# Splitting the decay scores of an RWKV-7 block into array quadrants, with two other pieces of work moved behind later steps

## The chip, the cores and the metric

The kernel runs on one core of one Trainium2 chip. The metric is the device time of one execution in microseconds. Before the change three runs gave 1024.06, 1024.72 and 1024.76 us, so the median is 1024.72 us.

## The reference, cut to what matters

One layer of a hybrid model works on 512 tokens of width 1024. It has a projection `w_in`, an RWKV-7 time mix with 16 heads of 64, a sliding-window attention, two gated output projections and a convolutional feed-forward block. The change sits in the time mix, whose recurrence is

```python
def step(S, inp):
    r_t, w_t, k_t, v_t, aa_t, bb_t = inp
    sa = jnp.einsum('bhvk,bhk->bhv', S, aa_t)
    S = S * w_t[:, :, None, :] + sa[..., None] * bb_t[:, :, None, :] + v_t[..., None] * k_t[:, :, None, :]
    y_t = jnp.einsum('bhvk,bhk->bhv', S, r_t)
    return S, y_t
...
y = (y - mean) * lax.rsqrt(var + GN_EPS)
y = y.reshape(B, T, RWKV_DIM) * lnx_w.astype(f32) + lnx_b.astype(f32)
bonus = jnp.sum(rh * kh * r_k.astype(f32), axis=-1, keepdims=True) * vh
y = (y + bonus.reshape(B, T, RWKV_DIM)) * g.astype(f32)
```

The kernel computes it in chunks of 128 tokens. Inside a chunk it needs, for each head, the scores of every key (the vectors b and k, scaled by decays) against every query (a and r, scaled likewise), kept only where the query is later than the key. The part of b against a is a triangular matrix N, and the kernel needs the inverse of (1 - N).

## The kernel before, in words

The heads are worked off two at a time, in eight pairs n = 0 to 7; head h of a pair lies on partitions 64h to 64h + 63. The 512 tokens are four chunks j. For each pair the kernel runs three stages, on TensorE (`pe`), VectorE (`dve`), ScalarE (`act`) and GpSimd (`pool`), each with an order written out by hand and semaphores between them:

- `scores(n)`: 16 fp32 matmuls (each shown in the profile as two passes) of a chunk's 128 keys (`bp` or `kp`, 64 rows) against its 256 queries (`ar`: 128 for a, then 128 for r). They fill the PSUM banks 0 to 5 and then 0 and 1 again. VectorE moves them out in eight `copy_predicated` under the mask `causal` (`masked`, L1532): `gb` holds the scores of b, `gk` those of k, and what the mask leaves out stays zero from one clearing at the start. TensorE also turns value, `bp` and `kp` chunks by transposes (`turned`, L2232).
- `invert(n)`: ScalarE copies N to fp16 (`n1`, `score_copy`, L1073), and GpSimd subtracts to get the rounding error (`n2`, `remainder`, L738). Then seven levels double the size of the inverted blocks of Y and of its transpose X. VectorE makes X's first level (`xx`, L1582) and Y's first level (`yy`, two masks, L1597); each later level is a product (L2351), a mask (`v1`, L1597), a product (L2374) and a sum (`yy`, L1608).
- `scan(n)`: the chain over the four chunks, run at the start of the next pair.

Between these pieces TensorE runs one k-step (three matmuls, L2046 to L2048) or two of the tiles of `w_in` that are still to be projected, by a table `FILL` of places ("scores", "centred", "tokens", (level, "masks"), ...). VectorE and ScalarE split those tiles' weights in high and low parts (L1357; in halves L1569 at levels 1, 2, 4 and 5).

The norm of the pair before (d = n - 1) is threaded through this. TensorE sums squares by row (`norm_var`, L2226), ScalarE takes the root (`deviation`: `brow` and `yrow`), TensorE turns it (`turned_var`, L2277), VectorE divides and spreads the result over 512 columns (`deviations`, L1520 and the copy L1507), TensorE turns it back (`deviations`, L2232 of `ysq`), and `scaled_output` uses it at level 3. GpSimd sends the bonus rows through DRAM and back (`bonus_back`: L814, L817), fetches the next key norms (`key_norms_in`, L808) and multiplies (L850).

Of the kernel before, what the change touches and what calls it, by code (L numbers as in the profile page):

```python
# [31 lines left out]
U32 = mybir.dt.uint32  # L32
# [22 lines left out]
SCORE_BANK = (0, 1, 2, 3, 4, 5, 0, 1)  # L55
# [67 lines left out]
def build(nc, x, norm1_g, w_in, rwkv_mu, w0, w2, a0, a2, g2, k_k, k_a, r_k, lnx_w, lnx_b,  # L123
          b_qkv, attn_sink, gate_b, w_proj_a, w_proj_b, w_out, norm2_g, w_up, conv_w,
          conv_b, w_down, normf_g, out):
    with ExitStack() as ctx:
# [149 lines left out]
        gb = take("gb", [P, NT, 2, 2 * C])  # L276
# [3 lines left out]
        gk = take("gk", [P, NT, 2, 2 * C])  # L280
# [356 lines left out]
        def _(pool):  # L637
# [98 lines left out]
            def remainder(n):  # L736
                pool.wait_ge(n1_ready, n + 1)
                pool.tensor_tensor(n2[:, :, :, :], gb[:, :, :, 0:C], n1[:, :, :, :], ALU.subtract)\  # L738
                    .then_inc(n2_ready, 1)
# [96 lines left out]
            for n in range(1, PAIRS):  # L836
# [6 lines left out]
                odd_columns(n)  # L843
                remainder(n)
                bonus_back(n - 1)
# [39 lines left out]
        def _(act):  # L885
# [185 lines left out]
            def score_copy(n):  # L1071
                act.wait_ge(g_ready, n * 8 + 4)
                act.activation(n1[:, :, :, :], gb[:, :, :, 0:C], ACT.Copy).then_inc(n1_ready, 1)  # L1073
# [277 lines left out]
        def _(dve):  # L1351
# [171 lines left out]
            def masked(n, f):  # L1523

                j0, h = (f % 4) // 2 * 2, f % 2
                dst = (gb, gk)[f // 4][:, j0:j0 + 2, h, :]
                if n == 0:
                    dve.wait_ge(cleared, 1 + f // 4)
                dve.wait_ge(g_ps, n * 8 + f + 1)

                dve.memset(carrier[:, f:f + 1], 0.0)
                dve.copy_predicated(dst, causal[:, :].bitcast(U32).unsqueeze(1)  # L1532
                                    .to_broadcast([P, 2, 2 * C]),
                                    ps[SCORE_BANK[f]][:, :].rearrange("p (j t) -> p j t", j=2))\
                    .then_inc(g_ready, 1)
# [42 lines left out]
            def invert(n, d, following):  # L1578
# [7 lines left out]
                for lv in range(LEVELS):  # L1586
                    for g in range(2):
                        dve.wait_ge(v_ps, n * (2 * LEVELS) + (2 * lv + g + 1))
                        vg = v1[:, 2 * g:2 * g + 2].rearrange("p j h t -> p (j h t)")
                        if lv == 0:  # L1590
# [126 lines left out]
            for f in range(8):  # L1717
                masked(0, f)
            value_tokens(0)
            invert(0, None, True)  # L1720
            for n in range(1, PAIRS):
# [305 lines left out]
        def _(pe):  # L2027
# [251 lines left out]
            def scores(n, d, fill):  # L2279
# [4 lines left out]
                for f in range(0, 8, 2):  # L2284
                    src, j0 = (bp, kp)[f // 4], f % 4
                    if f == 6:
                        pe.wait_ge(g_ready, n * 8 + 2)
                    for j in range(j0, j0 + 2):
                        for h in range(2):
                            hs = slice(h * HD, (h + 1) * HD)  # L2290
                            ins = pe.matmul(ps[SCORE_BANK[f + h]][:, (j - j0) * 2 * C:  # L2291
                                                                  (j - j0 + 1) * 2 * C],
                                            src[hs, j * C:(j + 1) * C], ar[hs, 1 - n % 2, j, :],
                                            start=True, stop=True)
                            if j > j0:
                                ins.then_inc(g_ps, 1)
                if d is not None:
# [16 lines left out]
            def invert(n, d, following, fill):  # L2314
# [20 lines left out]
                for lv in range(LEVELS):  # L2335
# [5 lines left out]
                    for g in range(2):  # L2341
# [415 lines left out]
```

## Time and profile before

| | us |
|---|---|
| median of three runs | 1024.72 |
| the profiled execution's own time | 1024.05 |
| its span, from the first to the last instruction | 1022.3 |
| TensorE busy | 1011.7 |
| VectorE busy | 738.1 |
| ScalarE busy | 516.2 |
| GpSimd busy | 224.4 |

The profile's times are counted from the start of the span; 1.75 us of the execution's own time lie outside it. In the timeline a row has its start, its length and the instruction, with the number of like instructions merged (x16) and, in brackets, the engine's idle time before it. A TensorE row's length includes the way through the array, so the rate of matmuls is read from one start to the next.

### The profile page before, as it was taken

How to read it: one execution, taken by the hardware profiler on the slowest of the kernel's cores; microseconds unless marked ns; L12 is line 12 of the kernel's file. 1: busy time of each engine (PE TensorE's matmuls, PEld its weight loads, DVE VectorE, ACT ScalarE, POOL GpSimd, SP SyncE). 2: the span in 40 equal slices, each digit the busy share in tenths (PEclk: the TensorE clock that was granted, in tenths of full speed). 3: DMA queues.
4: the chain of work that ended last, by engine and by line, in shares of the span. 5: the costliest groups of instructions: out<-in, count | busy, mean ns of one | idle time of the engine just before them, and what ended most of it. 6: DMA issues, size and time to landing. Idle time of an engine off the chain costs nothing.

```text
span 1022.3 us, 18746 instructions
## 1 busy us (share of the span) xinstructions
PE 1011.7 (99%) x7106; PEld 806.3 (79%) x7106; DVE 738.1 (72%) x1233; ACT 516.2 (50%) x869; POOL 224.4 (22%) x298
## 2 busy tenths in 40 slices
PE   8999999999999999999999999999999999999997
PEld 7888888777777777777777888888888888888886
DVE  5224667788988888888877565367767777789786
ACT  6435756844435445345453322264455444467744
POOL 7642355330221422413210554000000000000000
PEclk9999999999999999999999999999999999999999
DMA  6874456331303313214255867613233333337662
GB/s 187 233 236 153 132 191 215 94 76 43 86 25 74 86 63 87 61 60 120 93 164 153 238 234 258 198 40 103 85 102 92 95 100 103 92 114 226 203 189 113
DMA packets 161291, 133.25 MB, mean 130 GB/s; under 512 B 32729, under 2 KB 137735, under 8 KB 161223
## 3 DMA queue, kind: packets, MB, share of 16 engines
q1 hardware_dynamic: 147687, 88.41, 29.7%
q0 software_dynamic: 13520, 43.90, 13.9%
q8 instruction: 47, 0.77, 0.3%
q14 instruction: 21, 0.17, 0.0%
q10 hardware_dynamic: 16, 0.00, 0.0%
HBM read 111.83 MB, written 20.45 MB: 129 GB/s over the span
## 4 chain that ended last, share of the span: by engine, by line
PE 94%; DVE 2%; DMA 1%; issue 1%; ACT 1%; POOL 0%; SPq 0%; DVEq 0%; POOLq 0%; ACTq 0%
PE ps L2090 14%; PE ps L2093 14%; PE ps L2092 14%; PE ps L2046 6%; PE ps L2048 5%; PE ps L2047 5%; PE ps L2677 3%; PE ps L2678 3%; PE ps L2679 3%; PE ps L2291 3%; PE ps L2425 2%; PE ps L2232 2%; PE ps L2613 1%; PE ps L2611 1%; PE ps L2612 1%; PE ps L2374 1%
## 5 line engine op out<-in xcount | busy, mean ns | idle before, releaser
L1357 DVE TENSOR_TENSOR wlo<-raw,whi 128x1024 fp32r<-128x1024 f32 x106 | 140.1, 1322 | 125.9 <-ACT whi L893 108.0
L893 ACT ACTIVATE whi<-raw 128x1024 fp32r<-128x1024 f32 x116 | 122.6, 1057 | 127.0 <-PE ps L2093 116.0
L2090 PE MATMUL ps<-xnh,whi 128*128 128x512 f32 x336 | 130.7, 389 | 0.0
L2092 PE MATMUL ps<-xnl,whi 128*128 128x512 f32 x336 | 130.7, 389 | 0.0
L2093 PE MATMUL ps<-xnh,wlo 128*128 128x512 f32 x336 | 130.7, 389 | 0.0
L2046 PE MATMUL ps<-xh,whi 128*128 128x512 f32 x192 | 89.5, 466 | 0.0
L2090 PE MATMUL ps<-xh,whi 128*128 128x512 f32 x224 | 88.3, 394 | 0.0
L2092 PE MATMUL ps<-xl,whi 128*128 128x512 f32 x224 | 87.3, 390 | 0.0
L2093 PE MATMUL ps<-xh,wlo 128*128 128x512 f32 x224 | 87.2, 389 | 0.0
L2048 PE MATMUL ps<-xh,wlo 128*128 128x512 f32 x192 | 76.1, 396 | 0.0
L2047 PE MATMUL ps<-xl,whi 128*128 128x512 f32 x192 | 75.3, 392 | 0.0
L2090 PEld LDWEIGHTS ps<-xnh,whi 128*128 128x128 f32 x336 | 63.1, 188 | 13.2
L2092 PEld LDWEIGHTS ps<-xnl,whi 128*128 128x128 f32 x336 | 63.1, 188 | 13.2
L2093 PEld LDWEIGHTS ps<-xnh,wlo 128*128 128x128 f32 x336 | 63.1, 188 | 13.0
L1093 ACT ACTIVATE xx<-ps 128x256 f16<-128x256 f32 x96 | 32.1, 381 | 69.1 <-PE ps L2331 68.3
L2090 PEld LDWEIGHTS ps<-xh,whi 128*128 128x128 f32 x224 | 42.0, 188 | 10.1 <-issue 0.8
L2093 PEld LDWEIGHTS ps<-xh,wlo 128*128 128x128 f32 x224 | 42.1, 188 | 8.9
L2092 PEld LDWEIGHTS ps<-xl,whi 128*128 128x128 f32 x224 | 42.1, 188 | 8.4
L1879 DVE TENSOR_TENSOR sq<-ps,rs 128x512 f32<-128x512 f32 x44 | 30.4, 691 | 23.5 <-PE ps L2093 18.5
L745 POOL TENSOR_TENSOR z<-z,kmod 128x512 f32<-128x512 f32 x8 | 16.2, 2025 | 126.2 <-DVE kp L1488 126.2
L2048 PEld LDWEIGHTS ps<-xh,wlo 128*128 128x128 f32 x192 | 36.0, 188 | 8.3
L1608 DVE TENSOR_TENSOR yy<-ps,yy 128x256 f16<-128x256 f32 x96 | 36.2, 419 | 8.6 <-PE ps L2374 8.3
(430 smaller groups left out, 2454.6 us busy)
## 6 DMA issues: line engine op xcount, KB each, us to landing
raw<-in_w_in SPq DMA_DIRECT2D x108, 256.0 KB, 3.3
raw<-in_w_up SPq DMA_DIRECT2D x88, 256.0 KB, 3.0
wrow<-in_w_down POOLq DMA_DIRECT2D x22, 512.0 KB, 5.1
raw<-weight_scratch SPq DMA_DIRECT2D x44, 256.0 KB, 3.4
raw<-in_w_down SPq DMA_DIRECT2D x32, 256.0 KB, 2.9
weight_scratch<-wrow POOLq DMA_DIRECT2D x11, 512.0 KB, 3.1
gates_scratch<-gst POOLq DMA_DIRECT2D x16, 256.0 KB, 3.2
raw<-in_w_proj_b SPq DMA_DIRECT2D x16, 256.0 KB, 4.2
```

Of the source, the lines that this page charges most:

```text
L893: act.activation(flat(whi[:, hb]), flat(raw[:, b]), ACT.Copy).then_inc(w_hi, 1)
L1093: act.activation(dst, src, ACT.Copy).then_inc(x_ready, 1)
L1357: dve.tensor_tensor(flat(lo[:, hb]), flat(raw[:, b]), flat(hi[:, hb]).bitcast(F32), ALU.subtract).then_inc(w_lo, 1)
L1608: dve.tensor_tensor(yg, low_half(ps[2 * g][:, :], lv), yg, ALU.add)\
L2046: pe.matmul(o, whi[:, hb, k, :], self.hi(k), start=k == 0, stop=False)
L2047: pe.matmul(o, whi[:, hb, k, :], self.lo(k), start=False, stop=False)
L2048: ins = pe.matmul(o, wlo[:, hb, k, :], self.hi(k), start=False, stop=k == KT - 1)
L2090: pe.matmul(ps[bank][:, :], whi[:, hb, k, :], hi(k), start=first and k == 0, stop=False)
L2092: pe.matmul(ps[bank][:, :], whi[:, hb, k, :], lo(k), start=False, stop=False)
L2093: ins = pe.matmul(ps[bank][:, :], wlo[:, hb, k, :], hi(k), start=False, stop=last and k == kn - 1)
L2291: ins = pe.matmul(ps[SCORE_BANK[f + h]][:, (j - j0) * 2 * C: (j - j0 + 1) * 2 * C], src[hs, j * C:(j + 1) * C], ar[hs, 1 - n % 2, j, :], s ...
L2677: pe.matmul(o, h_hi, hi[:, cols], start=start, stop=False)
```

## The change

It has four parts.

1. The scores of the early 64 keys of a chunk against its early 64 queries (of a and r) become matmuls of 64 x 64 that lie in the four quadrants of the array: head h picks the rows, the parity e of the chunk picks the output partitions. They fill banks 2 and 3, for b and k together. The late 64 queries are scored against all 128 keys in banks 0, 1 (b) and 4, 5 (k). The early queries against the late keys, which the mask cleared, are not computed. No bank is used twice. There are 32 matmuls (64 passes) where there were 16 (32 passes), each with 128 moving columns instead of 256.
2. VectorE moves them out in eight `copy_predicated` again: four on 64 partitions for the early queries (two of these read partitions 64 to 127 and write 0 to 63), then two late ones for b, then the value tokens, then two late ones for k. All of b's scores are complete after the sixth, where they were after the fourth. In pair 0 the first of them waits until `gk` is cleared too.
3. The norm's division and its spreading (`deviations` on VectorE) move from between the masks to behind the two masks of Y's first level; TensorE's turning back moves from the scores to level 1, ahead of the fill (1, "masks"). `turned_var` moves behind the turns of values and `bp`.
4. GpSimd sends the bonus rows ahead of its subtraction, and the subtraction waits until X's first level is made (`x_start`).

```diff
+EARLY_BANK = (2, 3)
+LATE_BANK = ((0, 1), (4, 5))
...
-        gb = take("gb", [P, NT, 2, 2 * C])
+        gg = take("gg", [P, NT, 2, 2, 2, C])
+        gb, gk = (gg[:, 2 * i:2 * i + 2].rearrange("p x e h q t -> p (x e) h (q t)")
+                  for i in range(2))
...
             def remainder(n):
                 pool.wait_ge(n1_ready, n + 1)
+                pool.wait_ge(x_start, n + 1)
...
                 odd_columns(n)
+                bonus_back(n - 1)
                 remainder(n)
-                bonus_back(n - 1)
...
             def score_copy(n):
-                act.wait_ge(g_ready, n * 8 + 4)
+                act.wait_ge(g_ready, n * 8 + 6)
...
+            def late_masked(n, i, h):
+                f = 4 + 2 * i + h
                 if n == 0:
-                    dve.wait_ge(cleared, 1 + f // 4)
+                    dve.wait_ge(cleared, 1 + i)
                 dve.wait_ge(g_ps, n * 8 + f + 1)
...
+            def early_masked(n, h, e):
+                if n == 0:
+                    dve.wait_ge(cleared, 2)
+                dve.wait_ge(g_ps, n * 8 + 4)
+                predicated(gg[0:HD, :, e, h, :, 0:C // 2],
+                           two_parts(causal[0:HD, :], slice(0, C // 2)),
+                           ps[EARLY_BANK[h]][e * HD:(e + 1) * HD, :]
+                           .rearrange("p (x q t) -> p x q t", x=NT, q=2),
+                           None if h or e else 0)
...
+                    if lv == 0 and d is not None:
+                        deviations(d)
...
-                for f in range(6):
-                    masked(n, f)
-                deviations(n - 1)
-                for f in range(6, 8):
-                    masked(n, f)
+                masked(n, 0)
                 value_tokens(n)
+                masked(n, 1)
                 invert(n, n - 1, n < PAIRS - 1)
...
+                def late(i):
+                    src = (bp, kp)[i]
+                    for j in range(NT):
+                        for h, hs in enumerate(rows):
+                            ins = pe.matmul(ps[LATE_BANK[i][h]][:, j * C:(j + 1) * C]
+                                            .rearrange("p (q t) -> p q t", q=2),
+                                            src[hs, j * C:(j + 1) * C], both(hs, j, slice(HD, C)),
+                                            start=True, stop=True)
...
+                        for e in range(2):
+                            j = 2 * jj + e
+                            for h, hs in enumerate(rows):
+                                ins = pe.matmul(ps[EARLY_BANK[h]][e * HD:(e + 1) * HD, o:o + C]
+                                                .rearrange("p (q t) -> p q t", q=2),
+                                                src[hs, j * C:j * C + HD], both(hs, j, slice(0, HD)),
+                                                start=True, stop=True)
...
                 fill("scores")
-                if d is not None:
-                    turned_var(d)
-                pe.wait_ge(g_ready, n * 8 + 3)
+                pe.wait_ge(g_ready, n * 8 + 2)
                 turned(2, z[:, n + 16, :]).then_inc(tok_ps, 1)
                 pe.wait_ge(g_ready, n * 8 + 4)
                 turned(3, bp).then_inc(tok_ps, 1)
                 if d is not None:
-                    deviations(d)
+                    turned_var(d)
                 fill("centred")
-                pe.wait_ge(g_ready, n * 8 + 8)
+                pe.wait_ge(g_ready, n * 8 + 6)
                 turned(1, kp).then_inc(tok_ps, 1)
...
+                    if lv == 1 and d is not None:
+                        deviations(d)
                     fill((lv, "masks"))
```

## Rows read from the trace of the kernel before

**Rows 1.** The page, busy us of each engine and its instructions.

```profile
PE 1011.7 (99%) x7106; PEld 806.3 (79%) x7106; DVE 738.1 (72%) x1233; ACT 516.2 (50%) x869; POOL 224.4 (22%) x298
```

**Rows 2.** Timeline of TensorE in pair 4, from the scores to level 1.

```profile
376.24 2.00 PE L2291 MATMUL ps<-ar,bp 64*128 64x256 f32 x16
...
379.91 0.43 PE L2226 MATMUL ps<-ysq,meancols 128*32 128x128 f32 x8
380.15 0.40 PE L2226 MATMUL ps<-z,rkcols 128*32 128x128 f32 x8
...
382.32 0.66 PE L2232 MATMUL ps<-ident,ysq 128*128 128x128 f32 x4
382.74 0.48 PE L2046 MATMUL ps<-xh,whi 128*128 128x512 f32 x1
...
386.77 0.42 PE L2351 MATMUL ps<-yy,n 128*128 128x64 f16 x8
...
387.80 0.42 PE L2374 MATMUL ps<-v,xx 128*128 128x64 f16 x8
```

**Rows 3.** Timeline of VectorE in pair 4, from the first mask to level 1.

```profile
377.41 0.74 DVE L1532 COPY_PREDICATED gb<-causal,ps 128x512 f32<-128x512 uint32 x1 [0.29 <-issue]
...
380.57 0.75 DVE L1532 COPY_PREDICATED gk<-causal,ps 128x512 f32<-128x512 uint32 x1
...
381.60 0.21 DVE L1520 RECIPROCAL ystd<-ps 128x8 f32<-128x8 f32 x1 [0.28 <-PE ps L2277]
381.84 0.43 DVE L1507 COPY ysq<-ystd 128x512 f32<-128x512 f32 x1
...
383.50 0.67 DVE L1497 TENSOR_REDUCE vsum<-ps 128x8 f32<-128x512 f32 x1
...
384.81 0.69 DVE L1582 TENSOR_TENSOR xx<-n,first_level 128x1024 f16<-128x1024 f16 x1
385.41 0.78 DVE L1597 TENSOR_TENSOR yy<-ps,level_mask 128x256 f16<-128x256 f32 x2
...
388.80 0.68 DVE L1569 TENSOR_TENSOR wlo<-raw,whi 128x512 fp32r<-128x512 f32 x1
```

**Rows 4.** Timeline of TensorE, the attention's scores and the next product.

```profile
184.41 1.16 PE L2176 MATMUL ps<-kb,qc 64*128 64x128 f32 x16
185.51 0.50 PE L2090 MATMUL ps<-xh,whi 128*128 128x512 f32 x1
```

**Rows 5.** Timelines of VectorE and GpSimd where their instructions meet.

```profile
221.67 1.49 DVE L1582 TENSOR_TENSOR xx<-n,first_level 128x1024 f16<-128x1024 f16 x1
...
220.43 2.17 POOL L738 TENSOR_TENSOR n<-gb,n 128x1024 f16<-128x1024 f32 x1
...
160.91 1.63 DVE L1414 TENSOR_SCALAR nmx<-mx 128x8 f32<-128x8 f32 x1
...
161.20 1.30 POOL L781 TENSOR_TENSOR wrow<-wrow 128x512 f32<-128x512 f32 x1
```

**Rows 6.** Timeline of VectorE in pair 1, the last step before the masks.

```profile
254.67 0.75 DVE L1392 SCALAR_TENSOR_TENSOR z<-ps,par,z 128x511 f32<-128x511 f32 x1
...
255.33 0.74 DVE L1532 COPY_PREDICATED gb<-causal,ps 128x512 f32<-128x512 uint32 x1
```

**Rows 7.** Timeline of GpSimd in pair 4, the bonus rows.

```profile
384.27 0.56 POOL L814 DMA_DIRECT2D bonus_scratch<-brow  x1
386.38 1.26 POOL L817 DMA_DIRECT2D z<-bonus_scratch  x2 [1.54 <-DMA bonus_scratch<-brow]
...
392.03 1.29 POOL L850 TENSOR_TENSOR z<-z 128x512 f32<-128x512 f32 x1 [3.15 <-DMA z<-bonus_scratch]
```

**Rows 8.** Timeline of pair 0: the first mask, the clearing, level 1.

```profile
215.24 0.73 DVE L1532 COPY_PREDICATED gb<-causal,ps 128x512 f32<-128x512 uint32 x1
215.26 1.88 POOL L829 MEMSET gk<- 128x2048 f32 x1
...
223.84 0.44 PE L2351 MATMUL ps<-yy,n 128*128 128x64 f16 x8
```

More of the change, by code:

```diff
@@ L54 @@
 FILL_BANK = (7, 4, 7)
-SCORE_BANK = (0, 1, 2, 3, 4, 5, 0, 1)
+EARLY_BANK = (2, 3)
+LATE_BANK = ((0, 1), (4, 5))
 WARM = 24
@@ L279, in build @@
         ysb = take("ysb", [P, T])
-        gk = take("gk", [P, NT, 2, 2 * C])
         rkcols = take("rkcols", [P, P // NT])
@@ L1521, in deviations, with two_parts, predicated, masked @@
                 spread(ysq, ystd).then_inc(vex_ready, 1)
-            def masked(n, f):
-                j0, h = (f % 4) // 2 * 2, f % 2
-                dst = (gb, gk)[f // 4][:, j0:j0 + 2, h, :]
+            def two_parts(t, ts):
+                return t.rearrange("p (q t) -> p q t", q=2)[:, :, ts]
+            def predicated(dst, mask, scores, f=None):
+                if f is not None:
+                    dve.memset(carrier[:, f:f + 1], 0.0)
+                dve.copy_predicated(dst, mask.bitcast(U32).unsqueeze(1)
+                                    .to_broadcast([mask.shape[0], NT, 2, C // 2]), scores)\
+                    .then_inc(g_ready, 1)
+            def late_masked(n, i, h):
+                f = 4 + 2 * i + h
                 if n == 0:
-                    dve.wait_ge(cleared, 1 + f // 4)
+                    dve.wait_ge(cleared, 1 + i)
                 dve.wait_ge(g_ps, n * 8 + f + 1)
[L1531 to L1535, printed above, removed]
+                predicated((gb, gk)[i][:, :, h, :].rearrange("p j (q t) -> p j q t", q=2)
+                           [:, :, :, C // 2:], two_parts(causal[:, :], slice(C // 2, C)),
+                           ps[LATE_BANK[i][h]][:, :].rearrange("p (j q t) -> p j q t", j=NT, q=2), f)
+            def early_masked(n, h, e):
[7 more added lines that the diff above has]
+                           None if h or e else 0)
+            def masked(n, i):
+                if i == 0:
+                    for h in range(2):
+                        for e in range(2):
+                            early_masked(n, h, e)
+                for h in range(2):
+                    late_masked(n, i, h)
             def add_bonus(d):
@@ L1716, in _ @@
             weights(n + 2)
-            for f in range(8):
-                masked(0, f)
+            masked(0, 0)
             value_tokens(0)
+            masked(0, 1)
             invert(0, None, True)
@@ L2283, in scores, with both @@
                     pe.wait_ge(ps_free, N_FILL - 1)
[L2284 to L2293, printed above, removed]
+                rows = [slice(h * HD, (h + 1) * HD) for h in range(2)]
+                def both(hs, j, ts):
+                    return ar[hs, 1 - n % 2, j, :].rearrange("p (q t) -> p q t", q=2)[:, :, ts]
+                def late(i):
[5 more added lines that the diff above has]
+                                            src[hs, j * C:(j + 1) * C], both(hs, j, slice(HD, C)),
                                             start=True, stop=True)
-                            if j > j0:
+                            if j == NT - 1:
                                 ins.then_inc(g_ps, 1)
+                for i, src in enumerate((bp, kp)):
+                    for jj in range(2):
+                        o = (2 * i + jj) * C
+                        for e in range(2):
+                            j = 2 * jj + e
[4 more added lines that the diff above has]
+                                                start=True, stop=True)
+                                if i and jj:
+                                    ins.then_inc(g_ps, 1)
+                late(0)
+                late(1)
                 if d is not None:
```

## Prediction

> **What bounds the kernel now.** I read the page first: TensorE is busy 1011.7 us of a span of 1022.3 us [rows 1], so a change is worth what it takes from TensorE's own work, less what TensorE then has to wait. Next I read one pair in the timeline, engine by engine; pair 4 stands for pairs 3 to 7. On TensorE the scores start at 376.24, the variance products follow at 379.91, level 1's first product starts at 386.77 and its second at 387.80 [rows 2]. The reader is to see that each of these starts where the matmuls ahead of it end: nothing in this stretch waits for long. On VectorE the first mask starts at 377.41 and Y's first level ends at 386.19 [rows 3], 0.58 before level 1 needs it. VectorE is close behind TensorE all the way, and that is the margin which the change moves. The profiled execution took 1024.05 us by itself, 0.67 below the median of the runs; my sums are made against 1024.05.
>
> **Part 1, the quadrants.** Before, the 32 passes of the scores hold TensorE for 3.67 us (379.91 - 376.24) [rows 2], the change of tile shape behind them included. After, the 32 late passes have the shape of the attention's scores: 16 of those take 1.10 us to the next product's start [rows 4], of which I allow 0.2 for the change of shape between them, so 0.056 each and 1.8 us. The 32 early passes use half the rows and half the columns, and no row shows that. From below: the variance products use a quarter of the columns and eight of them take 0.24 us (380.15 - 379.91) [rows 2], so 0.03 each and 0.96 us. From above: no more than two at a time, 0.056 each, 1.8 us. I take 0.96, because the variance products show four streams at once and a quadrant needs four. With 0.4 for two changes of shape the scores take 3.16 us, which frees 0.51 us of each pair (with the upper bound they take 4.0, a loss of 0.3). The turning of `ysq`, 0.42 us (382.74 - 382.32) [rows 2], leaves this stretch and comes back at level 1.
>
> **Part 2, the masks.** Eight masks stay eight, at 0.63 us from start to start (five steps from 377.41 to 380.57) [rows 3]. The first early mask needs all 32 early passes, so it starts a little later: before, the first increment came with the sixth pass, which starts 5 x 0.11 = 0.55 after the first (3.67 / 32 = 0.11); after, the last comes with the 32nd, which starts 31 x 0.03 = 0.93 after the first. That is 0.38 later, less some 0.1 for a pass of half the columns, so the mask starts 0.28 later, at 377.69. In pairs 1 and 2 the first mask starts when the shift ends (255.33 against 255.42) [rows 6], and nothing is lost there. Two early masks read partitions 64 to 127, which no mask before does; I price that at nothing, by the nearest row, the masks that follow each other at 0.63, and keep as the upper bound the loss of the overlap of two neighbours (0.74 - 0.63 = 0.11) at each of four changes of partitions, 0.44 a pair.
>
> From there VectorE's chain in pair 4 is a plain sum. The sixth mask ends at 377.69 + 5 x 0.63 + 0.75 = 381.59; value tokens from 381.50, with 1.31 from their start to that of what follows (384.81 - 383.50) [rows 3]; masks 7 and 8 from 382.81, and X's first level from 384.10 to 384.79. The copy of N by ScalarE has to wait for mask 6 instead of mask 4, but X's first level comes 2.5 us later than that mask, so it is not late. Y's first level ends at 385.48. This is 0.7 us earlier than before, since the division has left the chain.
>
> **Parts 3 and 4, where they meet.** Now the division (0.21) and the spreading copy (0.43) [rows 3] stand behind Y's first level, and the copy would run from 385.64 to 386.07. But GpSimd's subtraction is released by X's first level, so it runs in the same stretch: from about 384.84 for 2.17 [rows 5], to 387.01. GpSimd is free for it: the variance products now end before 380, and the bonus rows need 2.11 + 1.26 = 3.37 us from first issue to the last one [rows 7], so they are sent off by 384.8 if they start by 381.4.
>
> What happens when VectorE and GpSimd meet is in [rows 5]. In pair 0 X's first level took 1.49 us instead of 0.69 [rows 3]; it started inside the subtraction and ended 0.56 behind its end (223.16 against 222.60). At 160.91 an instruction on eight columns with a single tensor took 1.63 us and ended with GpSimd's instruction (162.54 against 162.50). Both sat out GpSimd's work. The spreading copy is of the second kind: one tensor, SBUF to SBUF, and at 0.43 for 512 columns faster than the 0.68 of a two-tensor step of the same size [rows 3]. So I expect the copy to end at 387.01 + 0.30 = 387.31 (its 0.43 less the 0.13 which the held X also had behind it). The masks of level 1 read PSUM and stand behind it in VectorE's queue.
>
> The Trainium skill, "VectorE: DVE Perf Modes", section "Mode 2×_2P — use both read ports for one tensor", says that an fp32 copy within SBUF doubles its rate by using the second read port too, and its section "Two Vector instructions with no wait between them" calls that read interface shared with GpSimd. By that the copy is held as [rows 5] show for its neighbours; were a copy with a repeated source exempt, the sum would be that of the first rival.
>
> TensorE stands waiting for this copy at level 1: it reaches the place near 386.1 (386.77 less the 0.51 and 0.42 that left, plus some 0.25 for the product), and can turn `ysq` only after 387.31. From there the turn (0.42), the fill (1.03 from first to second product [rows 2], less the product) and a semaphore's way make 1.27; the second product starts at 388.58 against 387.80 [rows 2]: 0.78 us later in each of pairs 3 to 7, and 0.50 in pairs 1 and 2. The 0.51 us which the quadrants free is waited away there.
>
> **What comes late next.** GpSimd fetches key norms once `ysq` is turned (two issues like the 1.26 of [rows 7], from about 388.1) and then multiplies the bonus (1.29) from about 389.4; its rows have landed (5.65 us from the issue at 386.38 to 392.03 [rows 7], now issued near 382.8). Before, that multiplication ran at 392.03, away from any step it could hold. Now the half-weight split of level 1 comes at 388.58 + 1.00 = 389.6 (388.80 - 387.80) [rows 2, 3]: two SBUF tensors, like those held in [rows 5]. If GpSimd is first by these 0.2 us, the split ends 0.55 behind 390.7 instead of at 390.3; 0.95 late. Part of that is slack, as the 0.58 ahead of level 1 was; between nothing (with the split first, too) and 0.95 I take 0.7, since by the sum GpSimd is first, in pairs 1 to 6 (pair 7 fetches no key norms).
>
> **Pair 0** has no norm to divide, but its first mask now waits for the clearing of `gk`, until 215.26 + 1.88 = 217.14 instead of 215.24 [rows 8]. X's first level ends 7.1 us behind the first mask (384.79 - 377.69), at 224.3, Y's at 225.0; level 1's product comes at about 225.0 instead of 223.84: 1.2 us. The 0.8 us that X lost to the subtraction there is no gain, because TensorE did not wait for it.
>
> **The sum.** 5 x 0.78 + 2 x 0.50 + 6 x 0.7 + 1.2 = 10.3 us, so 1034.3 against 1024.05. I state 1034.5 for the measured median, between this and the same sum on 1024.72.
>
> **The rivals.**
> - *The split goes first.* Without the 0.7 at level 2: 6.1 us, 1030.2. For it: the lead is 0.2 us, within the error of a sum of seven durations. Against it: nothing shown.
> - *The copy is not held (the other side).* Then it ends at 386.07, the second product starts at 386.1 + 1.27 = 387.4, so 0.4 earlier in pairs 3 to 7 and 0.7 in pairs 1 and 2: 1.2 - 2.0 - 1.4 = -2.2, 1021.8. It decides as soon as the subtraction starts later than 385.6, that is when the bonus rows keep GpSimd until then, or when a copy can run beside GpSimd. Against it: both held steps of [rows 5]. With masks at their upper bound this case gives 1024.9, no change.
> - *Masks held at a change of partitions.* 0.44 in each of seven pairs on top of the forecast: 3.1, 1037.4. It delays the chain that sets the end, so it counts in full. The Trainium skill's "VectorE: DVE Perf Modes", section "Two Vector instructions with no wait between them", has such a rule: an instruction whose input starts in another quadrant of partitions than the last one waits until all before it are finished. No row here shows it.
> - *The quadrants overlap only two at a time.* The masks start 31 x 0.026 = 0.8 later in pairs 3 to 7: 4.0 more, 1038.3. Against it: the 0.03 of [rows 2].
>
> **How the numbers follow.** The forecast 36 in 100, the split first 24, the copy not held 28 (18 of these faster by over 0.2%, 10 within), masks held 6, two quadrants 6. A change of 0.2% is 2 us, about what these runs can tell. The range runs from 1022, which leaves out the better part of the second rival, to 1038, which leaves out the last: some 2 in 10 lie outside. The likeliest case's own range, with the split first or not and masks half held, is 1030 to 1036. So faster 0.18, within 0.2% 0.10, slower 0.72.
>
> **What the profile after will show.** Right: the scores about 0.5 us shorter; the spreading copy 1.6 us long instead of 0.43, ending with the subtraction; TensorE idle over 1 us ahead of turning `ysq` at level 1; in pairs 1 to 6 the first half-weight split longer than 0.68. Wrong: a copy of 0.43 beside the subtraction, or a subtraction that starts behind it; then the time falls below 1024. If the early passes start 0.056 apart, the last rival holds; if early masks start more than 0.7 apart, the third.

## The result and the profile after

The kernel got slower: 1043.80 us median (1042.49 to 1044.44, four runs) against 1024.74 us for the kernel before on the same chip, a ratio of 1.0186, 95% interval 1.0174 to 1.0198. The profiled execution took 1044.17 us, with a span of 1042.5. The prediction had the direction right, but said 1034.5 us with a range up to 1038: some 10 us more where 19 were measured.

The page of the kernel after, the line that answers to [rows 1]:

```profile
PE 1012.4 (97%) x7362; PEld 809.4 (78%) x7362; DVE 756.0 (73%) x1209; ACT 516.6 (50%) x869; POOL 223.3 (21%) x298
```

TensorE is as busy as before in a span that is 20.2 us longer, so it waits. VectorE is busy 18 us longer with 24 instructions fewer: single instructions of it have grown. Where TensorE waits, in the view of the waits (total, number, longest; the DMA's and other single waits of the start left out):

```profile
PE ps L2257 <- DVE ysq L1510: 11.7, 7, 2.0
PE ps L2416 <- DVE v L1623: 3.4, 5, 0.8
...
PE ps L2257 <- DVE gg L1532: 2.0, 2, 1.1
PE ps L2071 <- ACT n L1076: 1.8, 7, 0.4
```

Four waits: for the spread norm `ysq`, turned at level 1, in each of the seven pairs; for the mask `v` of level 2; for the masks of pair 0; and for ScalarE's copy of N. The last of them costs nothing, because it comes ahead of the wait for `ysq` in the same pair: without it TensorE would stand that much longer for `ysq`. The timeline of TensorE in pair 4 shows where they lie (it answers to [rows 2]):

```profile
386.40 0.67 PE L2331 MATMUL ps<-ar,bp 64*64 64x128 f32 x16
386.89 0.62 PE L2331 MATMUL ps<-ar,kp 64*64 64x128 f32 x16
387.43 1.16 PE L2318 MATMUL ps<-ar,bp 64*128 64x128 f32 x16
388.43 1.06 PE L2318 MATMUL ps<-ar,kp 64*128 64x128 f32 x16
389.42 0.43 PE L2251 MATMUL ps<-ysq,meancols 128*32 128x128 f32 x8
...
393.27 0.50 PE L2071 MATMUL ps<-xh,whi 128*128 128x512 f32 x1 [0.20 <-ACT n L1076]
...
397.99 0.66 PE L2257 MATMUL ps<-ident,ysq 128*128 128x128 f32 x4 [1.58 <-DVE ysq L1510]
...
399.19 0.41 PE L2416 MATMUL ps<-v,xx 128*128 128x64 f16 x8
...
402.44 0.62 PE L2416 MATMUL ps<-v,xx 128*128 128x64 f16 x8 [0.80 <-DVE v L1623]
402.90 0.47 PE L2071 MATMUL ps<-xh,whi 128*128 128x512 f32 x1
```

The scores did get shorter: 3.02 us from their start to the variance products (389.42 - 386.40) against 3.67. The 16 early passes of b take 0.49 us to those of k (386.89 - 386.40), 0.031 each. That is half of the 0.062 of a late pass of the same 128 columns ((388.43 - 387.43) / 16), whose 64 x 128 tile fits into the array twice; so four quadrants do run at once. But behind them TensorE stands 0.20, 1.58 and 0.80 us: 2.58 in this pair. VectorE in the same pair (answers to [rows 3]):

```profile
387.66 0.72 DVE L1532 COPY_PREDICATED gg<-causal,ps 64x512 f32<-64x512 uint32 x1 [0.38 <-issue]
...
388.41 2.29 DVE L1532 COPY_PREDICATED gg<-causal,ps 64x512 f32<-64x512 uint32 x3
...
390.74 1.38 DVE L1532 COPY_PREDICATED gg<-causal,ps 128x512 f32<-128x512 uint32 x2
...
394.64 0.65 DVE L1608 TENSOR_TENSOR xx<-n,first_level 128x1024 f16<-128x1024 f16 x1
395.23 0.76 DVE L1623 TENSOR_TENSOR yy<-ps,level_mask 128x256 f16<-128x256 f32 x2
395.90 0.17 DVE L1523 RECIPROCAL ystd<-ps 128x8 f32<-128x8 f32 x1
396.11 1.82 DVE L1510 COPY ysq<-ystd 128x512 f32<-128x512 f32 x1
...
400.19 1.86 DVE L1595 TENSOR_TENSOR wlo<-raw,whi 128x512 fp32r<-128x512 f32 x1
```

and GpSimd (answers to [rows 7]):

```profile
390.96 0.54 POOL L817 DMA_DIRECT2D bonus_scratch<-brow  x1 [1.23 <-ACT yrow L1047]
394.22 1.26 POOL L820 DMA_DIRECT2D z<-bonus_scratch  x2 [2.73 <-DMA bonus_scratch<-brow]
395.49 2.15 POOL L741 TENSOR_TENSOR n<-gg,n 128x1024 f16<-128x1024 f32 x1
...
400.19 1.31 POOL L853 TENSOR_TENSOR z<-z 128x512 f32<-128x512 f32 x1
```

Read the two side by side. The spreading copy (1.82 instead of 0.43) lies beside the subtraction and ends 0.29 behind it (397.93 against 397.64). The split (1.86 instead of 0.68) starts with GpSimd's multiplication and ends 0.55 behind it (402.05 against 401.50). TensorE waits for the copy itself, and behind the split for the mask `v`, which stands next in VectorE's queue. In all seven pairs the copy ends 0.28 to 0.29 behind the subtraction, so the start of the subtraction sets how long TensorE waits. The early masks are a second thing: from the first of them to the first late one 3.08 us pass in four steps (390.74 - 387.66), 0.77 each, against 0.63 before.

Windows of one pair, from scores to scores (us; busy time and instructions of PE, PEld, DVE, ACT, POOL; granted clock; DMA share; GB/s), first the kernel before, pair 4:

```profile
376.24:416.86 40.62, 40.62 (x477) 30.18 (x475) 34.31 (x82) 19.01 (x39) 10.95 (x13) 1.00 0.28 74
```

then the kernel after, pairs 4 and 5, and three stretches of 2 us at the wait in pair 5:

```profile
386.40:429.39 42.99, 40.37 (x509) 30.26 (x507) 37.05 (x79) 19.09 (x39) 11.08 (x13) 1.00 0.30 70
429.39:473.25 43.86, 41.63 (x508) 31.34 (x506) 36.81 (x79) 18.99 (x39) 11.05 (x13) 0.96 0.29 69
...
440.00:442.00 2.00, 0.56 (x3) 0.57 (x4) 2.00 (x3) 0.00 (x0) 1.09 (x1) 0.89 0.49 61
442.00:444.00 2.00, 2.00 (x14) 1.39 (x13) 0.04 (x1) 0.00 (x0) 1.24 (x2) 0.50 0.09 29
444.00:446.00 2.00, 2.00 (x24) 1.58 (x22) 1.98 (x4) 0.32 (x2) 1.30 (x1) 0.75 0.84 57
```

Before, TensorE had no idle time in the pair at all. After, 2.62 of 42.99 us. Pair 5 lost more: TensorE was busy for 0.56 of the 2 us in which it waits for `ysq`, the granted clock then stood at 0.50 (the 1.2 GHz level) for the next 2 us and came back in the two behind them, and the pair's matmuls took 1.26 us more of busy time than those of pair 4. In pair 2 it fell to 0.50 behind the wait too; the other pairs read 1.00, the 2.4 GHz level.

### The profile page after: what moved, and what is told of

Same layout as the page of the kernel before. It is cut to its first block, busy times and chain, and to the rows that moved or that the text cites. A ratio compares the mean times of both kernels' runs of the same rounds, so it can differ in the third digit from the quotient of the medians.

```text
span 1042.5 us, 19242 instructions
## 1 busy us (share of the span) xinstructions
PE 1012.4 (97%) x7362; PEld 809.4 (78%) x7362; DVE 756.0 (73%) x1209; ACT 516.6 (50%) x869; POOL 223.3 (21%) x298
## 4 chain that ended last, share of the span: by engine, by line
PE 84%; DVE 10%; issue 3%; DMA 1%; ACT 1%; POOL 0%; SPq 0%; DVEq 0%; POOLq 0%; ACTq 0%
PE ps L2115 14%; PE ps L2117 14%; PE ps L2118 14%; PE ps L2071 5%; PE ps L2073 4%; PE ps L2072 4%; PE ps L2719 3%; PE ps L2720 3%; PE ps L2721 3%; DVE gg L1532 2%; PE ps L2416 1%; PE ps L2655 1%; PE ps L2653 1%; PE ps L2654 1%; DVE ysq L1510 1%
## 5 line engine op out<-in xcount | busy, mean ns | idle before, releaser
L2115 PEld LDWEIGHTS ps<-xh,whi 128*128 128x128 f32 x224 | 42.0, 188 | 10.2 <-issue 0.8
L1532 DVE COPY_PREDICATED gg<-causal,ps 64x512 f32<-64x512 uint32 (+1 forms) x64 | 45.8, 739 | 4.8 <-issue 1.9
L2118 PEld LDWEIGHTS ps<-xh,wlo 128*128 128x128 f32 x224 | 42.1, 188 | 8.8
L2071 PEld LDWEIGHTS ps<-xh,whi 128*128 128x128 f32 x192 | 37.0, 193 | 9.3 <-ACT n L1076 3.7
```

Of the source, the lines that this page charges most:

```text
L1532: dve.copy_predicated(dst, mask.bitcast(U32).unsqueeze(1) .to_broadcast([mask.shape[0], NT, 2, C // 2]), scores)\
L2071: pe.matmul(o, whi[:, hb, k, :], self.hi(k), start=k == 0, stop=False)
L2115: pe.matmul(ps[bank][:, :], whi[:, hb, k, :], hi(k), start=first and k == 0, stop=False)
L2118: ins = pe.matmul(ps[bank][:, :], wlo[:, hb, k, :], hi(k), start=False, stop=last and k == kn - 1)
```

## The experiments

Theory P (port): the copy and the split are long because GpSimd works on SBUF beside them. Theory Q (place): they come late because of where they stand in VectorE's queue, and would whatever GpSimd does. Beside these, the held masks and the clearing in pair 0 had to be sized. In the diffs, minus is the kernel that is named.

**e1_one_step**, the kernel after with division and spreading in one instruction that reads PSUM:

```
-                chain(dve.reciprocal(by_token(ystd[:, :]), by_token(ps[6][:, P:2 * P])))
-                spread(ysq, ystd).then_inc(vex_ready, 1)
+                dve.reciprocal(ysq[:, :].rearrange("p (j h v) -> p j h v", j=NT, h=2),
+                               by_token(ps[6][:, P:2 * P]).unsqueeze(3)
+                               .to_broadcast([P, NT, 2, HD])).then_inc(vex_ready, 1)
```

> The changed kernel, with VectorE's division and spreading done by one reciprocal that reads PSUM with a repeated source, in the same place. Theory (the spreading copy is held by GpSimd's subtraction): a PSUM source is not held, so the step takes about 0.7 us instead of 0.17 + 1.82, TensorE's wait ahead of turning ysq falls from 1.58 to about 0.3 us in pairs 1 to 7, and the time falls by 8 to 9 us, to about 1035. Rival (the place in VectorE's queue costs the time, the hold is a by-product): TensorE still waits over 1 us there and the time stays within 2 us of 1043.8.

Measured: 1056.20 us, ratio 1.0316 (1.0298 to 1.0335). This told nothing between the theories, because the instruction is long by itself (view by line, minimum, median and maximum in ns):

```profile
L1523 DVE RECIPROCAL ysq<-ps x8: 3331/3342/3354, 265.9 to 570.1; 128x512 f32<-128x512 f32 x8
```

All eight take 3.3 us, the one behind the last pair too. The instruction for all columns costs more than a reciprocal of 8 columns and a held copy together (0.17 + 1.82).

**e2_multiply_later**, the kernel after with GpSimd's multiplication held until the first half-split is through:

```
                 pool.wait_ge(bonus_in, 32 * n)
+                pool.wait_ge(w_lo, N_FILL + 3 * n + 2)
```

> The changed kernel, with GpSimd's bonus multiplication waiting until VectorE has split the second half of the first tile's weights (level 2). Theory (the multiplication holds the first half-weight split, 1.86 us instead of 0.68 in pair 4): the split takes 0.68 in all pairs, TensorE's wait ahead of level 2's second product (0.80) goes, and the time falls by about 0.95 in six pairs, 5.7 us, to about 1038. Rival (the level is late for another reason): the split is short, but the time stays within 2 us of 1043.8.

Measured: 1036.20 us, 1.0121 (1.0104 to 1.0138). VectorE in pair 4:

```profile
392.38 1.90 DVE L1511 COPY ysq<-ystd 128x512 f32<-128x512 f32 x1
...
396.54 0.68 DVE L1596 TENSOR_TENSOR wlo<-raw,whi 128x512 fp32r<-128x512 f32 x1
```

The split, at its old place in VectorE's queue, is back at 0.68 us, TensorE's waits for `v` are gone, and 7.6 us with them (5.7 were expected). The copy, whose neighbour on GpSimd was not touched, stays at 1.90. For the split this is theory P.

**e3_scores_alone**, quadrant scores and masks only; division, turn, subtraction and bonus rows at their places of before (the edits to the kernel after; on TensorE both turns go back as well):

```
-                pool.wait_ge(x_start, n + 1)
...
-                bonus_back(n - 1)
                 remainder(n)
+                bonus_back(n - 1)
...
-                    if lv == 0 and d is not None:
-                        deviations(d)
...
                 masked(n, 0)
+                deviations(n - 1)
                 value_tokens(n)
...
```

> The quadrant scores and their masks alone; the division stays among the masks (behind the sixth), TensorE's turns, the subtraction and the bonus rows stay where they were before the change. Theory (the loss is made by the two moves): pair 0 loses 1.6 us to the clearing, pairs 1 to 7 gain some 0.1 each, since masks at a change of partitions (0.77 us apart instead of 0.63) give back what TensorE gains; 1022 to 1028. Rival (the quadrant scores or their masks make most of the loss): 1035 or more.

Measured: 1027.21 us, 1.0028 (1.0018 to 1.0038). **e4_moves_alone**, the kernel before with the moves and without the quadrants:

```
-                for f in range(6):
-                    masked(n, f)
-                deviations(n - 1)
-                for f in range(6, 8):
+                for f in range(8):
                     masked(n, f)
...
+                    if lv == 0 and d is not None:
+                        deviations(d)
...
+                pool.wait_ge(x_start, n + 1)
...
+                bonus_back(n - 1)
                 remainder(n)
-                bonus_back(n - 1)
...
```

(TensorE's two turns move with them, as in the change.)

> The kernel before, with the scores and masks as they were and only the two moves made: division behind Y's first level, bonus rows ahead of the subtraction, the subtraction behind X's first level. Theory (the moves make the loss): the spreading copy is held by the subtraction where that starts first, and the half-weight split by the multiplication; 1.2 to 1.5 us in each of seven pairs, 1033 to 1036. Rival (only scores and masks cost): 1023 to 1027.

Measured: 1037.47 us, 1.0131 (1.0110 to 1.0153), a little over the expected range. So the moves alone cost 13 us, and the quadrants, which shorten the scores, alone cost 2.9; the other 3 us of the 19 come only with both. Pair 4 of e3 in the windows:

```profile
378.69:419.34 40.65, 39.89 (x509) 30.04 (x507) 34.72 (x79) 19.04 (x39) 10.98 (x13) 1.00 0.28 74
```

TensorE's work has fallen by 0.73 us (40.62 to 39.89), but 0.76 of idle time has come: TensorE wants `ysq` sooner, while VectorE, with its masks at 0.77, ends the copy 0.23 later behind the start of the scores than before (waits of 5.8 us in seven pairs), and pair 0 waits 2.0 for its masks. In e4 VectorE and GpSimd meet as in the kernel after. Its VectorE, pair 4:

```profile
389.66 1.78 DVE L1508 COPY ysq<-ystd 128x512 f32<-128x512 f32 x1
...
393.71 1.85 DVE L1570 TENSOR_TENSOR wlo<-raw,whi 128x512 fp32r<-128x512 f32 x1
```

In one pair of this run, pair 2, the bonus rows kept GpSimd until the copy had begun. VectorE, and then GpSimd:

```profile
306.82 0.48 DVE L1508 COPY ysq<-ystd 128x512 f32<-128x512 f32 x1
```

```profile
307.09 2.21 POOL L739 TENSOR_TENSOR n<-gb,n 128x1024 f16<-128x1024 f32 x1
```

The copy, first by 0.27 us, took 0.48, TensorE did not wait for it, and the pair is 40.60 us long, where pairs 1 and 3 to 6 of the same execution have 42.46 to 43.21.

**f1_psum_spread**, the kernel after with the eight inverses written to PSUM and spread from there:

```
-                chain(dve.reciprocal(by_token(ystd[:, :]), by_token(ps[6][:, P:2 * P])))
-                spread(ysq, ystd).then_inc(vex_ready, 1)
+                inverse = ps[6][:, 3 * P:3 * P + 2 * NT]
+                chain(dve.reciprocal(by_token(inverse), by_token(ps[6][:, P:2 * P])))
+                dve.tensor_copy(ysq[:, :].rearrange("p (u v) -> p u v", v=HD),
+                                inverse.unsqueeze(2).to_broadcast([P, 2 * NT, HD]))\
+                    .then_inc(vex_ready, 1)
```

> The changed kernel, but the reciprocal writes its eight values to PSUM and the spreading copy reads them there, so that it is no longer a copy from SBUF to SBUF; its place in VectorE's queue, GpSimd's subtraction and all else stay. If the copy lasts 1.8 us because the subtraction runs beside it and both want SBUF (port theory), it now takes about 0.7 us (the half-split between tiles of the same size took 0.68), TensorE's wait of 1.58 us for ysq falls to about 0.4, and seven pairs give back 1.1 us each: 1036 us. If the place in the queue costs this anyway, TensorE waits as long as in the changed kernel and the time stays within 2 us of 1043.8. The split should stay at 1.86 us in both.

Measured: 1030.54 us, 1.0057 (1.0041 to 1.0074). VectorE in pair 3 of f1:

```profile
348.86 0.69 DVE L1525 COPY ysq<-ps 128x512 f32<-128x512 f32 x1
...
351.81 1.85 DVE L1598 TENSOR_TENSOR wlo<-raw,whi 128x512 fp32r<-128x512 f32 x1
```

and GpSimd there:

```profile
348.18 2.13 POOL L741 TENSOR_TENSOR n<-gg,n 128x1024 f16<-128x1024 f32 x1 [1.16 <-DVE xx L1611]
...
351.80 1.30 POOL L853 TENSOR_TENSOR z<-z 128x512 f32<-128x512 f32 x1
```

The copy from PSUM lies whole inside the subtraction (348.18 to 350.31) and takes 0.69 us: what it cannot share here is the reading of SBUF, since the place, the neighbour and the output are the same. The gain of 13 us is more than expected, and the split did not stay at 1.86 everywhere as expected. It comes 1.1 us earlier, and in pairs 2, 4, 5 and 7 the multiplication still waits for its rows from DRAM (4.2 us together), so that the split is first and takes 0.68. In pairs 1, 3 and 6 the two start within 0.01 us of each other. In pairs 1 and 3 the split is held, and these two pairs are 1.0 to 1.4 us longer than pairs 2 and 4 to 6 (42.07 and 41.89 against 40.70 to 40.90); in pair 6 it is not.

**f2_both**, f1 and e2 together:

> As f1, and GpSimd's multiplication of the bonus waits until the first half-split of the pair is through. Port theory: both long operations are gone (copy about 0.7, split 0.68), so the gains of the two add up, 7.7 of this one and the 7.6 that the later multiplication alone gave back: 1029 us, what is left over the kernel before being pair 0 and the masks. Place theory: 1036, as with the later multiplication alone.

Measured: 1027.02 us, 1.0026 (1.0016 to 1.0036). 16.8 of the 19 us are back with the copy and the split both left undisturbed.

**g2_subtract_later**, the kernel after with one wait more; the copy stays in SBUF and in its place:

```
                 pool.wait_ge(x_start, n + 1)
+                if n:
+                    pool.wait_ge(vex_ready, n)
```

> The changed kernel, with GpSimd's subtraction waiting until the spreading copy of the pair is through; the copy still goes from SBUF to SBUF and keeps its place in VectorE's queue. Port theory: the copy is back at 0.43 us, TensorE's wait for ysq falls from 1.6 to about 0.2, and the multiplication behind the subtraction comes too late for the first half-split, so about 2 us a pair come back in seven pairs: 1029 to 1031. If the place in the queue or the kind of output costs the time, the copy stays at 1.8 us and the time within 2 us of 1043.8. A later subtraction could also make TensorE wait for n; then the time would lie between, with that wait shown.

Measured: 1025.47 us, 1.0010 (1.0001 to 1.0020): below the expected interval. VectorE in pair 4 of g2:

```profile
387.38 0.43 DVE L1512 COPY ysq<-ystd 128x512 f32<-128x512 f32 x1
...
390.07 0.68 DVE L1597 TENSOR_TENSOR wlo<-raw,whi 128x512 fp32r<-128x512 f32 x1
```

and GpSimd:

```profile
387.99 2.13 POOL L743 TENSOR_TENSOR n<-gg,n 128x1024 f16<-128x1024 f32 x1 [0.96 <-DVE ysq L1512]
...
391.38 1.29 POOL L855 TENSOR_TENSOR z<-z 128x512 f32<-128x512 f32 x1
```

A wait that starts the subtraction a microsecond or two later brings back 18.3 us. The copy is 0.43 again, and the later subtraction pushes the multiplication behind the split. TensorE waits 0.2 a pair for `ysq`. Theory Q is out: the place in the queue is that of the kernel after. Pairs 1 to 6 are each 0.02 to 0.18 us shorter than in the kernel before; what is left over it is pair 0, 1.6 us longer.

**f3_mask_order**, the kernel after with the four early masks in the other order, so that the partitions they read change twice instead of four times up to the late masks:

```
-                    for h in range(2):
-                        for e in range(2):
+                    for e in range(2):
+                        for h in range(2):
...
-                pe.wait_ge(g_ready, n * 8 + 2)
+                pe.wait_ge(g_ready, n * 8 + 3)
```

(TensorE may write over bank 2 only after both of its masks, and the second of them is now the third in the queue.)

> The changed kernel, with the four early masks taken in the other order, so that VectorE changes between partitions 0 to 63 and 64 to 127 once between them instead of three times. If a mask that starts at a change of partitions is held by about 0.14 us, two of the three intervals fall from 0.77 to 0.63, mask 6 ends 0.28 earlier in each pair, TensorE's later waits with it: about 2 us, 1041.8. If the change of partitions costs nothing and 0.77 is what a mask takes, all intervals stay at 0.77 and the time stays at 1043.8.

Measured: 1041.72 us, 1.0169 (1.0152 to 1.0186), so 2.1 less, as expected, though the intervals of the two kernels overlap. The masks themselves settle it:

```profile
386.70 0.73 DVE L1532 COPY_PREDICATED gg<-causal,ps 64x512 f32<-64x512 uint32 x1 [0.38 <-issue]
...
387.33 2.11 DVE L1532 COPY_PREDICATED gg<-causal,ps 64x512 f32<-64x512 uint32 x3
...
389.48 1.38 DVE L1532 COPY_PREDICATED gg<-causal,ps 128x512 f32<-128x512 uint32 x2
```

The step from the first mask to the second, now on the same partitions, is 0.63 (387.33 - 386.70) and the four steps take 2.78 us instead of 3.08: two changes of partitions less are 0.15 each. By the trace, pairs 1 to 4 and 6 are 0.16 to 0.38 us shorter than in the kernel after.

**g3_clear**, the kernel after with the clearing moved into the attention's last stretch:

```
             attention_out(6)
+            pool.wait_ge(o_ps, 16)
+            pool.memset(gk[:, :, :, :], 0.0).then_inc(cleared, 1)
             attention_out(7)
             pool.wait_ge(ops_ready, 1)
-            pool.memset(gk[:, :, :, :], 0.0).then_inc(cleared, 1)
```

> The changed kernel, with the clearing of GpSimd's tile moved out of pair 0 into the last stretch of the attention. If pair 0 loses its 1.6 us to the masks that wait for the clearing, 1.2 to 1.6 us come back: about 1042.4. If the masks at the changes of partitions make it, at most 0.5 us come back: 1043.4.

Measured: 1043.42 us, 1.0189 (1.0168 to 1.0210): by the time not to be told from the kernel after. By the trace pair 0 is 39.94 us long instead of 41.82, and TensorE's waits for its masks fall from 2.0 to 0.3; but pair 5 of this execution, with a granted clock of 0.96, is 44.09 us long, and its four runs lie as far apart as 1041.8 and 1045.3. That the clearing makes pair 0 late is shown by the trace, its worth in the median not.

**f4_scores_turn_late**, quadrant scores, the other mask order, the earlier clearing, and `ysq` turned one group later, behind `kp`; everything else as before. To the edits of e3, f3 and g3 it adds:

```
                 turned(3, bp).then_inc(tok_ps, 1)
-                if d is not None:
-                    deviations(d)
...
                 turned(1, kp).then_inc(tok_ps, 1)
+                if d is not None:
+                    deviations(d)
```

> Quadrant scores with the masks in the other order, the division straight behind mask 6 and the subtraction and the bonus rows in their places of before; TensorE turns the statistics one group later, and the clearing of GpSimd's tile is moved from the first pair's start to the end of the attention. With the scores alone 1027.2 was measured, TensorE waiting 1.0 a pair for ysq and 2.0 in pair 0 for masks. If these waits are what eats the 0.5 us that the quadrants free in each pair, some 0.6 a pair come back and 1 us in pair 0: 1021 to 1022, under the kernel before. If the masks themselves set the time, 1025 to 1027.

Measured: 1021.94 us, 0.9974 (0.9961 to 0.9986). It beats both kernels. Pair 4 in the windows:

```profile
375.59:415.66 40.07, 39.96 (x509) 30.14 (x507) 34.45 (x79) 19.00 (x39) 10.99 (x13) 1.00 0.29 75
```

TensorE is idle 0.11 us in the pair, and the pair is 0.55 shorter than before: the whole gain of the quadrants. Two controls. **g4_scores_order_clear**, without the later turn:

> The candidate without the later turn of the statistics: quadrant scores, masks in the other order, clearing earlier, the division behind mask 6. From 1027.2 with the scores alone, two of three holds of the masks less (0.28 a pair) and about 1 us in pair 0 give 1024 to 1024.5, TensorE still waiting some 0.5 a pair for ysq; the later turn then brought the rest to 1021.9. If the order of the masks is worth nothing, it stays at 1026.

Measured: 1023.02 us, 0.9988 (0.9978 to 0.9998), a little under the expected 1024. By the trace the later turn is worth 0.15 to 0.35 us in each of pairs 1 to 6; the intervals of the two runs overlap. **g1_turn_late_before**, the later turn and the earlier clearing on the kernel before:

> The kernel before, with two edits of the best candidate alone: TensorE turns the statistics one group later, and GpSimd's tile is cleared in the attention's last stretch. It is the control for the candidate's 1021.9. In the kernel before TensorE waits nowhere for the statistics, and 0.2 us once for the cleared tile, so if the candidate's gain comes from the quadrant scores this stays at 1024.5, within 0.7 us. If the gain comes from the later turn and the earlier clearing, this too is at 1022.

Measured: 1027.93 us, 1.0036 (1.0024 to 1.0048), a miss: the edits don't leave the kernel before as it is, they cost it 3.5 us. One wait is new in all seven pairs, and pairs 1 to 6 are 0.30 to 0.43 us longer:

```profile
PE ps L2233 <- DVE gk L1533: 3.5, 7, 0.5
```

Before, turning `ysq` filled 0.42 us in which TensorE would have stood for the mask ahead of `kp`. Without it there TensorE stands. With the quadrants the turn of `kp` needs six masks instead of eight, TensorE does not stand for them, and the same move pays. The gain of f4 is the quadrants', in an order that fits them.

## Why the prediction was wrong

Right in its own steps: the scores (3.02 us, said 3.16), the early passes (0.031, said 0.03), the subtraction beside the copy, the copy's end (0.29 behind the subtraction, said 0.30), TensorE idle over 1 us ahead of turning `ysq` (1.58), the split held by the multiplication (0.55 behind it, as said). e2, f1, f2 and g2 show the mechanism that the forecast chose, and the trace of the kernel after excludes the rivals "copy not held" and "split goes first". What failed is the size: by the trace the span grew by 20.2 us, the sum had 10.3. The greater part of the difference has come by level 1's second product, and two terms ahead of it were mis-sized, the early masks and the bonus rows.

- *"Two early masks read partitions 64 to 127 ... I price that at nothing."* This step failed. The four changes cost 0.56 us a pair (3.08 - 4 x 0.63), more than the upper bound of 0.44. The first early mask came 0.19 sooner than forecast, so X's first level ended 8.89 us behind the start of the scores in pair 4, where the forecast has 8.55. By the prediction's own sign, early masks more than 0.7 apart, the third rival holds, with 6 chances in 100. The Trainium skill's "VectorE: DVE Perf Modes", section "Two Vector instructions with no wait between them", has the rule: an instruction whose input starts in another quadrant of partitions than the last one waits until all earlier ones have finished. The traces of f3 and of the kernel after agree, at 0.14 to 0.15 us a change. f3 shows what two of the four changes were worth: 0.29 to 0.38 us in pairs 1, 2, 3 and 6, but 0.16 in pair 4, where the bonus rows were the later ones.
- *"... the bonus rows need 2.11 + 1.26 = 3.37 us from first issue to the last one [rows 7], so they are sent off by 384.8 ..."* This step failed too. They started early enough (4.56 us behind the scores), but took 3.34 to 4.99 us, and in pairs 4 to 7 the subtraction started only when their last issue was over. The way through DRAM had been read from one pair. Already in the kernel before it took 3.37 us in pairs 3 to 6, 3.74 and 4.12 in pairs 1 and 2, and 4.43 in pair 7. The kernel after, in us behind the start of the pair's scores:

| pair | X's first level ends | last bonus issue ends | subtraction starts | TensorE waits for `ysq` |
|---|---|---|---|---|
| 1 | 9.10 | 8.32 | 9.25 | 1.49 |
| 2 | 9.12 | 8.67 | 9.56 | 1.77 |
| 3 | 8.93 | 7.90 | 9.08 | 1.50 |
| 4 | 8.89 | 9.08 | 9.09 | 1.58 |
| 5 | 8.92 | 9.54 | 9.56 | 2.02 |
| 6 | 8.87 | 9.02 | 9.03 | 1.53 |
| 7 | 8.89 | 9.35 | 9.35 | 1.84 |

Pair 5, where the rows were latest:

```profile
437.68 1.25 POOL L820 DMA_DIRECT2D z<-bonus_scratch  x2 [3.20 <-DMA bonus_scratch<-brow]
438.95 2.14 POOL L741 TENSOR_TENSOR n<-gg,n 128x1024 f16<-128x1024 f32 x1
```

In pairs 1 and 3 the subtraction follows X's first level by 0.15, so there the masks made it late. In pairs 4 and 6 both came at nearly the same time, and either alone would have made it nearly as late. In pairs 5 and 7 the rows made it later still. In pair 2 the trace shows no reason for the last 0.3. No run varies the way of the bonus rows alone.

- *"In pairs 1 and 2 the first mask starts when the shift ends ..., and nothing is lost there."* That held for the first mask (1.46 us behind the scores, before and after), but not for those behind it: level 1 of pair 1 was 1.09 us late, where 0.50 had been given, and the pair lost as much as the others (2.32).
- *The clock* was not in the sum. In pairs 2 and 5 it fell behind TensorE's wait, and with the later subtraction that made level 1 of these two 2.20 and 2.60 us later than before, where it is 1.09 to 1.23 in pairs 1, 3, 4 and 6. Some of it was won back at level 2, where TensorE did not have to wait; the pairs are 0.6 and 0.85 us longer than the others. These waits were the longest of pairs 1 to 6, but behind the 1.84 of pair 7 the clock stayed at 1.00; why it fell behind two of the seven stays open.
- *"... between nothing (with the split first, too) and 0.95 I take 0.7, since by the sum GpSimd is first ..."* The split cost 0.95 at the second product of level 2 in pair 4 (402.44 - 386.40 = 16.04 us after the scores, against 390.10 - 376.24 = 13.86 before, less the 1.23 of level 1). No slack took part of it up. That GpSimd was first is partly luck: in pairs 1, 3, 4 and 6 the two started within 0.01 us of each other, not 0.2 apart, and the last section shows such a tie that went the other way. In pair 7, priced at nothing, the split was held too, for 0.32 at level 2.
- *The product at level 2 itself* was not in the sum. It took 0.46 us to the next start (402.90 - 402.44) instead of the 0.24 of the kernel before:

```profile
390.10 0.41 PE L2374 MATMUL ps<-v,xx 128*128 128x64 f16 x8
390.34 0.48 PE L2046 MATMUL ps<-xh,whi 128*128 128x512 f32 x1
```

- *Pair 0* was 1.59 longer, said 1.2. The scores also started 0.96 later behind the attention; that start lies between 213.6 and 216.0 in the executions here, so I don't put it down to the change.

Stage by stage, the traces put the missing time at 6.1 us up to level 1's second product (3.5 of it in pairs 2 and 5), 1.4 from there to level 2's, 1.1 behind it, 0.4 in pair 0 and 1.0 ahead of it: the difference of 20.2 and 10.3, but for rounding. The range failed for one reason more: its upper end was each rival by itself. Yet even the masks and the split at their upper bounds together give 1034.3 + 3.1 + 1.5 = 1038.9; the rest was in no term. What the runs bring back (7.6 for the split, 9.2 more for the copy, 18.3 for the one wait of g2) holds the follow-up costs too: no pair of g2 shows a lower clock, and its masks are no faster. One pointer in the prediction is wrong: were a copy with a repeated source exempt, the sum would be that of the second rival, not of the first.

## What to carry to other kernels

When work is moved, ask what the other engines do at the new place. In this kernel a VectorE copy or split that read SBUF beside a GpSimd instruction lasted until that one was over. Let one wait for the other, or read from PSUM: here one wait was worth 18 us of 19. When a stage is made shorter, look at which wait the shortened stretch had been hiding and move the work that is not urgent behind it; the same later turn of `ysq` made the pairs longer in one kernel and shorter in the other. In a forecast, read a way through DRAM in every pair and not in one, since a step can hang on the latest; and add up the upper bounds of all small terms on the chain once, and let the range reach there at the least.

## What was not expected of the hardware

A reciprocal of 128 x 512 took 3.33 us, where one of 128 x 8 takes 0.2 and a copy of 128 x 512 from PSUM 0.69.

A spreading copy from PSUM isn't disturbed by GpSimd (0.69 inside the subtraction), while the faster one from SBUF is (0.43 alone, 1.78 to 2.06 in pair 4 of the kernels where it meets it).

The hold goes both ways. In pair 6 of f1 the split and the multiplication start at the same time. VectorE, and then GpSimd:

```profile
475.11 0.68 DVE L1598 TENSOR_TENSOR wlo<-raw,whi 128x512 fp32r<-128x512 f32 x1
```

```profile
475.11 1.84 POOL L853 TENSOR_TENSOR z<-z 128x512 f32<-128x512 f32 x1
```

Here the split keeps its 0.68 us and the multiplication takes 1.84 instead of 1.29, 0.55 more. In pair 4 of the kernel after, with both at 400.19, it was the other way, and TensorE paid: at a start that is the same to 0.01 us, the traces show both outcomes, and not what decides.
